# Moving the first chunk of expert work of a fused decoder layer into its last routing groups

## The reference, cut to what matters

```python
hf = rmsnorm(x, g)                                   # (1088, 1024)
lg = hf @ w_group                                    # 4 groups: the best one is taken
le = (hf @ w_expert) of the 8 experts in that group  # the best two are taken
gate_w = softmax(top 2 of le) * softmax(lg)[best group]
act = silu(hf @ w_gate[e]) * (hf @ w_up[e])          # 32 experts, each 1024 -> 256
out = sum over the token's two experts of gate_w * (act @ w_down[e])   # 256 -> 1024
y = rmsnorm(x + out, g_final)
```

## Time and profile before

| | us |
|---|---|
| median of 3 runs | 1110.55 |
| lowest and highest | 1109.17 and 1110.76 |
| profiled execution | 1114.35 |
| its span, first to last instruction | 1112.6 |
| PE busy | 1065.3 (96%) |
| DVE busy | 698.6 (63%) |
| ACT busy | 289.7 (26%) |
| POOL busy | 185.6 (17%) |

### The profile page before, as it was taken

One profiled execution on the slowest core, in us unless ns is written; L12 is line 12 of the kernel. 1 busy time (PEld: TensorE's weight loads), 2 busy tenths in 40 slices (PEclk: granted clock), 3 DMA queues, 4 the chain that ended last, 5 costly groups with the idle time before them and its releaser, 6 DMA issues.

```text
span 1112.6 us, 15646 instructions
## 1 busy us (share of the span) xinstructions
PE 1065.3 (96%) x6175; PEld 610.9 (55%) x6175; DVE 698.6 (63%) x1353; ACT 289.7 (26%) x587; POOL 185.6 (17%) x227
## 2 busy tenths in 40 slices
PE   6999999999999999999999999999999999999992
PEld 4666766787754445888766645554733333333330
DVE  5576699947858654743476686675643645555555
ACT  5200341567821111100033201111312222222232
POOL 5000100101000000000000000000122454554455
PEclk9999999999999999999999999999899999999997
DMA  9109550297645004100334450026789999999962
GB/s 302 48 1 207 50 42 1 91 285 244 224 164 174 1 1 177 50 1 1 129 136 160 182 189 39 38 73 223 260 280 403 412 410 413 414 415 412 412 223 82
DMA packets 75468, 204.97 MB, mean 184 GB/s; under 512 B 25592, under 2 KB 34448, under 8 KB 67056
## 3 DMA queue, kind: packets, MB, share of 16 engines
q1 hardware_dynamic: 54336, 168.82, 43.1%
q0 software_dynamic: 20928, 35.09, 9.3%
q10 hardware_dynamic: 128, 0.03, 0.0%
HBM read 195.23 MB, written 52.18 MB: 222 GB/s over the span
## 4 chain that ended last, share of the span: by engine, by line
PE 77%; DMA 7%; DVE 7%; issue 5%; ACT 3%; POOL 1%; ACTq 0%; another core or an unknown queue 0%; POOLq 0%; DVEq 0%
PE bank L809 16%; PE bank L981 9%; PE bank L1353 9%; PE bank L1046 9%; PE bank L1176 6%; PE bank L1371 4%; DMA arena<-work_firsts,ptmp 3%; PE bank L779 3%; PE bank L940 3%; PE bank L1078 3%; PE bank L1143 2%; DMA arena<-work_rows,slots_in 2%; DMA work_firsts<-arena,slots_in 2%; PE bank L1341 1%; PE bank L1220 1%
## 5 line engine op out<-in xcount | busy, mean ns | idle before, releaser
L809 PE MATMUL bank<-arena 128*128 128x360 f32 (+1 forms) x576 | 179.6, 472 | 0.9 <-DVE arena L1806 0.9
L1353 PE MATMUL bank<-arena 128*32 128x512 f32 x1536 | 170.0, 594 | 0.9 <-DVE arena L2536 0.9
L809 PEld LDWEIGHTS bank<-arena 128*128 128x128 f32 x576 | 109.4, 192 | 65.7 <-issue 3.1
L2125 DVE TENSOR_TENSOR arena<-arena,bank 128x512 f32<-128x512 f32 (+3 forms) x56 | 68.4, 1221 | 66.1 <-PE bank L1046 37.4
L1353 PEld LDWEIGHTS bank<-arena 128*32 128x32 f32 x1536 | 47.4, 110 | 105.1 <-issue 103.9
L981 PE MATMUL bank<-arena 128*128 128x272 f32 x448 | 103.0, 392 | 0.0
L1176 PE MATMUL bank<-arena 128*128 128x512 f32 x224 | 100.6, 597 | 1.0 <-DVE arena L2290 1.0
L1046 PE MATMUL bank<-arena 128*128 128x512 f32 x224 | 97.7, 593 | 0.0
L981 PEld LDWEIGHTS bank<-arena 128*128 128x128 f32 x448 | 85.0, 190 | 17.4
L1371 PE MATMUL bank<-arena 128*32 128x512 f32 x768 | 88.3, 592 | 0.0
L1455 ACT ACTIVATE arena<-bank 128x272 f32<-128x272 f32 (+5 forms) x94 | 41.9, 451 | 171.9 <-PE bank L809 123.8
(11 more groups left out here) (454 smaller groups left out, 1467.4 us busy)
## 6 DMA issues: line engine op xcount, KB each, us to landing
arena<-in_w_gate SPq DMA_DIRECT2D x32, 1024.0 KB
arena<-in_w_up SPq DMA_DIRECT2D x32, 1024.0 KB
arena<-in_w_down SPq DMA_DIRECT2D x32, 1024.0 KB
arena<-in_ck SPq DMA_DIRECT2D x8, 1024.0 KB, 7.1
arena<-in_cv SPq DMA_DIRECT2D x8, 1024.0 KB, 5.4
arena<-in_w_in SPq DMA_DIRECT2D x3, 2048.0 KB, 14.1
work_firsts<-in_x SPq DMA_DIRECT2D x1, 4352.0 KB
arena<-in_x SPq DMA_DIRECT2D x8, 512.0 KB, 6.0
```

Of the source, the lines that this page charges most:

```text
L809: last = nc.tensor.matmul(b[:, 0:w], win[slot][:, k, m * P:m * P + P], ht[:, k, c0:c0 + w], start=k == 0, stop=k == KD - 1)
L1353: last = nc.tensor.matmul(bank[2 + j % 2][t0:t0 + QT, :].rearrange("p (h n) -> p h n", h=2), xgt[j % 2][:, k, t0:t0 + QT], gu[e % GUB][:, ...
L2125: V.tensor_tensor(out, out, bank[banks(n)][:, :].unsqueeze(1).to_broadcast([P, width, 512]), ADD).then_inc(sem["md_free"], 1)
```

## The change

Chunk 0 now takes two quarters of expert 0 and two of expert 1, with the first `HEAD` = 64 rows of each, and only rows of the first six tiles (groups 0 to 2). Chunk 1 has the last quarter of expert 0, the last of expert 1 and two of expert 2. Rows of later tiles are placed behind: `heads_full` raises the running counts of experts 0 and 1 to at least 64 after group 2, for which PE counts once more (`early_totals`), and `chunk_place` shifts rows to their changed chunk. `role` compares places anew.

Chunk 0's index is written and its rows are gathered once group 2 is placed; its transposes, gate/up, product and down stand between the index matmuls of the last two groups, and the fillers there are now 4, 6, 4 and 8. On DVE `main_rows(0)` goes between `choose(4)` and `place(4)`, and the product of chunk 0 ahead of `role(3)`. On ACT silu and copy of chunk 0 go ahead of the exponentials. POOL gathers chunk 0, then after the index chunks 1, 2 and 3. The round loops start at chunk 1; the weights of experts 5 and 6 are both requested after `gate_up(1)`, those of down after `down(1)`.

```diff
+        EARLY = len(GROUPS) - 2
+        A_OK = [g + 1 + (g >= EARLY) for g in range(NGR)]
+        HEAD = 64
+        def expert_of(j, t):
+            return ((0, 0, 1, 1), (0, 1, 2, 2))[j][t] if j < 2 else (4 * j + t) // 3
+        def last_round(e):
+            return max(1, (3 * e + 2) // 4)
...
SP
-                    if (3 * e + 2) // 4 == j:
+                    if last_round(e) == j:
                         sp.wait_ge(sem["gu_full"], j + 1)
                         load_gu(e + GUB, e % GUB, sem[f"gu_in{e % GUB}"])
...
-                    if (3 * e + 2) // 4 == j - 1:
+                    if last_round(e) == j - 1:
...
POOL
-            pool.wait_ge(sem["xn2_st0"], 80)
-            pool.wait_ge(sem["xn2_st1"], 64)
+            pool.wait_ge(sem["xn2_st0"], 48)
+            pool.wait_ge(sem["xn2_st1"], 48)
             pool.wait_ge(sem["idx_ok"], 1)
...
-            fetch(0, 0, "xg_in0")
-            nc.gpsimd.memset(xg[1][:, D - 4:RW], 0.0).then_inc(sem["pool_own"], 1)
-            pool.wait_ge(sem["pool_own"], 19)
+            fetch(0, 0, "xg_in0", 2 * EARLY * P)
+            pool.wait_ge(sem["xn2_st0"], 80)
+            pool.wait_ge(sem["xn2_st1"], 64)
+            pool.wait_ge(sem["idx_ok"], 2)
             fetch(1, 1, "xg_in1")
+            fetch(2, 2, "xg_in2")
...
PE
+            def early_totals():
+                pe.wait_ge(sem["a_ok"], EARLY + 1)
+                nc.tensor.matmul(bank[6][:, 2 * P:2 * P + 2], ones[:, :], ac[:, 0:2], start=True, stop=True).then_inc(sem["rk_full"], 1)
...
             b = out_product(3, "m3", 0, 2)
+            early_totals()
             raw_t(8)
...
             keep_busy(4)
             router(6)
+            pe.wait_ge(sem["tp_free"], tp.n + 1)
+            rows_t(0, 0, "xg_in0", 16, "t_full", None)
             index_ends(3, 0)
             keep_busy(6)
             rank(4)
             totals()
-            keep_busy(8)
+            pe.wait_ge(sem["t_free"], 2)
+            pe.wait_ge(sem["ma_free"], ma.n + 1)
+            gate_up(0, 0, 6)
             index_ends(4, 0)
-            keep_busy(7)
+            gate_up(0, 6, KD)
+            keep_busy(4)
+            pe.wait_ge(sem["prod_ok"], 1)
+            prod_t(0, "ht_full")
+            pe.wait_ge(sem["htm_ok"], 1)
+            pe.wait_ge(sem["a_ok"], A_OK[-1] + 1)
+            down(0)
             index_ends(3, 1)
             index_ends(4, 1)
             keep_busy(8)
...
-            rows_t(0, 0, "xg_in0", 16, "t_full", None)
-            pe.wait_ge(sem["t_free"], 2)
-            gate_up(0, 0, 4)
             rows_t(1, 1, "xg_in1", 16, "t_full", 1)
-            gate_up(0, 4, KD)
-            for j in range(NR):
+            pe.wait_ge(sem["t_free"], 4)
+            gate_up(1, 0, 4)
+            rows_t(2, 2, "xg_in2", 16, "t_full", 3)
+            gate_up(1, 4, KD)
+            for j in range(1, NR):
...
DVE
+            def chunk_place(g):
+                n = len(GROUPS[g])
+                p_, at = pos[:, GROUPS[g][0]:GROUPS[g][0] + n, :], moved[:, 0:n, :]
+                if g >= EARLY:
+                    return p_
+                t = [turn[:, k, 0:n, :] for k in range(3)]
+                link(V.tensor_scalar(t[0], p_, float(P + HEAD), float(HEAD), ALU.is_ge, MUL), V.tensor_scalar(t[1], p_, float(P + CAP), -float(CAP), ALU.is_ge, MUL),
+                     V.tensor_scalar(t[2], p_, float(P + CAP + HEAD), float(CAP - HEAD), ALU.is_ge, MUL))
+                link(V.tensor_tensor(at, p_, t[0], ADD), V.tensor_tensor(t[1], t[1], t[2], ADD))
+                link(V.tensor_tensor(at, at, t[1], ADD))
+                return at
+            def heads_full():
+                dve.wait_ge(sem["rk_full"], EARLY + 1)
+                link(V.tensor_tensor(bump[:, 4:6], bump[:, 0:2], bank[6][:, 2 * P:2 * P + 2], SUB))
+                link(V.tensor_tensor(bump[:, 4:6], bump[:, 4:6], bump[:, 2:4], ALU.max))
+                link(V.tensor_tensor(ac[0:1, 0:2], ac[0:1, 0:2], bump[0:1, 4:6], ADD))
...
place:
+                if g == EARLY - 1:
+                    V.tensor_copy(bump[:, 4:6], bump[:, 0:2]).then_inc(sem["a_ok"], 1)
...
role:
-                link(V.scalar_tensor_tensor(key, over[:, 0:n, :], float(-2 * NE), eid[:, t0:t0 + n, :], MUL, ADD))
+                if g < EARLY:
+                    link(V.tensor_tensor(k_, moved[:, 0:n, :], e_, SUB))
+                    link(V.scalar_tensor_tensor(k_, k_, -8192.0, over[:, 0:n, :], ADD, MUL))
+                    link(V.tensor_tensor(k_, k_, e_, ADD))
...
             collect(2)
+            V.tensor_scalar(idxg[:, 0:1], acc[:, 0:1], float(EMPTY), None, ADD).then_inc(sem["idx_ok"], 1)
+            heads_full()
             out_add(3, 7)
...
             choose(4)
+            main_rows(0)
             place(4)
+            dve.wait_ge(sem["rk_full"], A_OK[-1] + 1)
+            V.scalar_tensor_tensor(cnt[:, 0, :], iota[:, 0:NE], float(-CAP), bank[5][:, 0:NE], MUL, ADD).then_inc(sem["a_ok"], 1)
...
+            dve.wait_ge(sem["silu_ok"], 1)
+            product(0, "prod_ok")
             role(3)
             role(4)
...
-            main_rows(0)
             dve.wait_ge(sem["ix_full"], NGR)
```

184 lines of the change are left out of this document (100 added, 84 removed).

## The result

The kernel after takes **1120.02 us** (median of 7 runs, 1117.22 to 1126.27) against 1110.60 (7 runs on the same chip, 1109.17 to 1113.61): ratio 1.0093, 95% interval 1.0066 to 1.0121. The forecast was 1114.2 with a range up to 1120.0. The side was right, the size was not: 9.4 us slower instead of 3.6. The profiled execution took 1120.64 us (span 1118.9), against 1114.35 (span 1112.6) before.

The account below looks back on a forecast made before the run. PE was taken to set the pace, with DMA at its limit beside it in the expert rounds. PE path 2.2, DMA 1 and chunk 4's gather 0.4 sum to +3.6 us on 1110.55: 1114.2, range 1107.5 to 1120.

Parts of the forecast that it names:

- The path up to chunk 3: PE's work from the routers to chunk 3's transposes: 2.2 us longer, ending at 826.4 against 824.17.
- Ahead of the last router: Added DVE steps in the early groups, early_totals and choose(3): 3.1 us more before the last router ends.
- The low clock at 792 to 799: Old trace's clock fall comes 3.1 us later, lasting 6.9 us; index_ends(4,0) ends 7.5 us later.
- the clock does not fall: Rival: wide matmuls replacing fillers and waits keep the clock up after the last router; -2.6 us, 1111.6; chance 0.15.
- The gather of chunk 0: Issued some 10 us before PE needs the rows, so hidden: nothing taken, 2 us kept for the range.
- The new wait: PE idles 3.3 us ahead of chunk 1's gate/up, until DVE's index and weight chain and row scaling end.
- the clock falls in the new gap: Rival: chunk 1's gate/up runs at 1.2 GHz after PE's idle gap; 1.7 to 3.4 us, 1116 to 1117.6; chance 0.11.
- Behind it: After chunk 3's start: 1 us for later weight requests of experts 5 and 6, 0.4 for chunk 4's gather.
- a sign of being wrong: The prediction called itself wrong if, among other signs, the late waits changed by more than 3 us.
- DMA becomes the bound: Rival: of 8 us of transfers put behind, weight slack hides some; 5 us more, 1119; chance 0.14.
- The carry-over: The profiled execution's 3.8 us above the median of the kernel before was taken to hold for both kernels.
- The faster rival: Gathers come in time in the rounds, removing 5 us of late waits and 1.4 for DMA; 1107.8; chance 0.18.

Follow-up runs that it names:

- b_late_slot: Kernel before, with only expert 5's weight requests moved to where the kernel after has them; ratio 1.0008.
- b_steps: Kernel before, with dummy DVE steps like the change's added ones in place and role for groups 0 to 2; ratio 1.0052.
- a_no_steps: Kernel after, without the added DVE steps of the first three groups (results not the layer's); ratio 1.0043.
- a_gap_fill: Kernel after, with 14 more fillers on PE in the gap ahead of chunk 1's gate/up; ratio 1.0048.
- a_rows_first_nokb: Kernel after, with chunk 1's rows scaled ahead of DVE's index chain and without eight fillers ahead of chunk 1's transposes; ratio 1.0071.
- a_light: Kernel after, loading one of eight slices of the gate and up weights of experts 5 and 6 (3.7 MB less); ratio 1.0050.
- a_we_light: Kernel after, with row weights computed early and 3.7 MB less gate and up weights of experts 5 and 6; ratio 1.0004.
- b_light: Kernel before, loading one of eight slices of the gate and up weights of experts 5 and 6 (3.7 MB less); ratio 0.9999.
- a_weights_early: Kernel after, with DVE's row weights and overflow counts moved ahead of its wait for the last index columns; ratio 1.0032.
- b_steps_fill7: Kernel before, with the dummy DVE steps of b_steps and six fillers on PE ahead of router(7)'s wait; ratio 1.0047.
- a_we_fill7: Kernel after, with row weights computed early and six fillers on PE ahead of router(7)'s wait; ratio 1.0017.
- a_we_no_steps: Kernel after, with row weights computed early and the added DVE steps of the first three groups taken out; ratio 0.9990.
- (after): The kernel after itself, without further edits, against the kernel before; 1120.02 us, ratio 1.0093.
- a_fill_light: Kernel after, with 14 fillers in the gap ahead of chunk 1's gate/up and 3.7 MB less weights of experts 5 and 6; ratio 1.0030.
- a_rows_first: Kernel after, with chunk 1's rows scaled ahead of DVE's chain of indices, counts and weights; ratio 1.0065.

## Why the prediction was wrong in size

**The path up to chunk 3** came out by errors that cancel. Predicted +2.2, measured +1.7 (825.84 against 824.17). The agreement is luck, for the 824.17 itself belongs to an execution with two low-clock stretches; against the 819.27 of b_late_slot, the same work of PE without them, the kernel after is 6.6 us late there.

- *Ahead of the last router*, +3.1 forecast. The two waits rose by 1.20 and 1.26, as written (to 2.17 and 1.80, forecast 2.2 and 1.9), and early_totals takes 0.28 us. The router itself is only 1.7 late, because the low clock at 768 to 772 of the earlier trace rows is absent. That low clock was worth (1 - 0.57) x 4 = 1.7 us, so 3.4 was spent ahead of the router (0.5 of it stands there at 726 us already, ahead of both waits). Right, as far as these two traces show; b_steps and a_no_steps say that over many executions the same steps cost 5.6 to 5.8 us (0.0050 and 0.0052), for in a part of the executions a low-clock stretch of some 11 us follows. The prediction priced these waits only by their length, and this consequence was not in its sum: **a term left out**, about 3 us by these runs (5.6 to 5.8 against the 2.4 to 2.5 of the two waits).
- *The low clock at 792 to 799*, failed. I moved the fall of the earlier trace rows along with the work. In the profile of after the stretch is at 1.00. Index_ends(4,0) is hence 3.5 us later (798.64 against 795.11), not 7.5; 1.4 of the 4.0 between them is the router's, which is 1.7 and not 3.1 late, the rest the clock's. The rival "the clock does not fall", with 0.15 and 2.6 us less, had this part.
- *The gather of chunk 0*: hidden, as written; it is issued at 778.53 and chunk 0's transposes wait for nothing.
- *The new wait*, right in place and cause and nearly in size: 3.85 us for 3.3 forecast, ended by DVE's row scaling behind a chain of 5.2 us. What the forecast left out of its sum is what this wait did to the clock. **That is the first step that failed.** The rival "the clock falls in the new gap" had it, with 0.11: priced at up to 3.4 us, measured 2.9 in the one half (6.57 against 3.64) and 5 us of the total by a_gap_fill (uncertain by 3.8). I argued against it from waits of 0.81 and 0.94 us that kept the clock; a wait of 3.85 is not near those rows, and a_rows_first_nokb shows a fall behind a wait of 0.94 us, so a short wait was no safe sign either. The Trainium skill, TensorE: Matmul & The Clock Gate, Part 1, calls the slow clock the default that activity lifts. The profile of after agrees (0.50 from 814 to 820 behind the gap), and it should have weighed more than two short waits.

**Behind it**, +1.4 forecast (1 for DMA, 0.4 for the fourth gather), measured +2.7 in the rounds and +1.9 after them. **This is the second step that failed**: the mechanism was right (requests after chunk 1's gate/up, an idle DMA before, more waits late), the term too small. It is 4.8 us by a_light and 3.1 by a_we_light. I took a value by the 4.7 us of all late waits, which were waits for rows (and 0.81 of them stood ahead of the rounds); the waits that grew are for weights, which had none before. PE's waits for DMA from 815 us on went from 3.9 to 7.8 us, more than the 3 us that the prediction named as a sign of being wrong. Its time for expert 6's old request, 820.7, was early: the profile of before has 822.27. The rival "DMA becomes the bound", 5 us, had the size. DMA is no bound in the kernel before, as b_light (0.9999) and b_late_slot (1.0008) show.

**The carry-over** of 3.8 us failed too. I took the distance of the profiled execution from the median as common to both kernels. That profile holds two low-clock stretches, worth 4.9 us on PE's path by b_late_slot, and by the mean clock most executions of the kernel before (29 of 35) seem to be without their like. The kernel after's profile has neither of them; its low clock stands behind a gap that its order of work makes. Its profiled execution is 0.6 us above its median, so of the 9.4 us between the medians 3.2 (3.8 - 0.6) are in no step of the sum.

**The terms**, each by the run that takes it out of the kernel after (0.001 is 1.1 us): gap, slow clock and late row weights 6.8 us (a_weights_early); added steps 5.6 (a_no_steps); late weight data 4.8, or 3.1 once the gap is closed. Each is uncertain by 3 to 4 us. The smallest sum, 6.8 + 5.6 + 3.1 = 15.5, is more than the loss of 10.3 by the ratio, which says that chunk 0's new place by itself would win some 5 us. No run took out all three, so this figure is an estimate and not shown, and its uncertainty is as large as itself. What is shown is the 3.3 us (uncertain by 2.4) between b_steps_fill7 and a_we_fill7, at equal steps and with the late requests still in. Without the steps the win is smaller and not clear of nothing: a_we_no_steps is at 0.9990. The faster rival, in which the late waits go, did not happen.

## What to carry to other kernels

When work is moved ahead of a chain that it used to cover, look at what the chain then leaves bare on the engine that sets the pace, and order the chain so that only what the next product needs stands in it: here the row weights, which needed nothing late, were worth 6.8 us (uncertain by 4) by their place alone. A new wait on a busy TensorE, here of 1.8 to 3.85 us, is to be priced with the low clock that can follow it, over many executions and not from one profile; fillers in the wait lowered the time in the kernel after (a_gap_fill), took the upper group away there (a_we_fill7, its ratio within the uncertainty), and did not measurably help in the kernel before (b_steps_fill7). Where a buffer's reader is moved to a later round, its next load moves too; compare the DMA rate just behind that point with the one before.

## What the runs showed of the hardware that I had not expected

With the same wait at one place the clock falls in one execution and not in another. Behind a wait of 1.75 to 1.81 us at router(7) the profiles of a_gap_fill, b_steps and a_weights_early have 11 us at a granted clock of 0.53 to 0.54; those of (after), a_light, a_fill_light, a_rows_first, a_rows_first_nokb and a_we_light, with the same wait, have 1.00 there. The first three, and none of the others, also fell behind the wait of 2.17 us at the last pair (0.50 at 738 to 740 us), whose first product took 5.37 us instead of 3.67. This is a_weights_early's chain of work that ended last (start, us):

```profile
736.27 5.37 PE bank L1196 x8
```

The two stretches are worth 1.7 us there and 4.9 from router(7) to the next router (14.2 us in a_gap_fill, 9.3 in the kernel after), 6.6 together. That is about the distance between the two groups of times: 5 to 7 us between their means in each kernel that has them, the kernel after among them (a_weights_early: six up to 1112.9, six from 1117.7). It fits that the upper group is these executions, but only one execution of each kernel was profiled. With the steps that lengthen the waits taken out, or with the wait at router(7) filled, no second group shows in 36 executions of three versions of the kernel after (a_no_steps 1114.4 to 1117.9, a_we_no_steps 1108.5 to 1112.4, a_we_fill7 1110.5 to 1115.4). In the kernel before with the same filler, b_steps_fill7, one of seven is still that long. Why the clock falls in one execution and not in the next stays open.

A fall also depends on the execution where no kernel differs: the stretches of low clock in the profile of before are in b_light's profile too, but not in b_late_slot's, in which PE's work up to 800 us is the same. PE waited 0.54 us for router(7) ahead of the first of them in the profile of before, and 0.54 us in b_late_slot's.

Nor does one length of wait bring one length of low clock: behind the same 3.85 us ahead of chunk 1, PE's first half took 6.57 us in the kernel after and 5.34 in a_no_steps, where the clock was back at 816 us.
